# One decoder layer with 32 experts: two parked weight loads in place of one, a shorter path through routing, gates behind bank reads, the output phase on four PSUM banks

## The chip, the cores and the metric

The kernel runs on one core of a Trainium2 chip. The metric is the device time of one execution in microseconds (us). A core has TensorE for matmuls (PE; its loads of the stationary operand are shown as PEld), VectorE (DVE), ScalarE (ACT), GpSimd (POOL) and SyncE (SP). Here SP does nothing but issue the big weight transfers, in the order of its program, each when the buffer it writes is free. A label such as SPq means the sequencer of that engine. All numbers are float32, so the work is dominated by reading some 450 MB of weights.

## The reference, cut to what matters

```python
mod = silu(c) @ w_ada + b_ada                      # six (D,) vectors a sequence: sh1 sc1 g1 sh2 sc2 g2
h = rms_norm(x, norm1_g) * (1 + sc1) + sh1         # 256 prompt tokens, 8 sample tokens, D = 1024
hq, hf, hi, hg, gq, gk, gv, gg, gr = split(h @ w_in)   # HGRN2 and GLA heads
o_h = rms_norm(gated_recurrence(silu(hq), k_h, hi, log_f)) * silu(hg)
o_g = rms_norm(gated_recurrence(gq, gk, gv, log_a)) * silu(gg)
x = x + g1 * (concat(o_h, o_g) @ w_o)
h = rms_norm(x, norm2_g) * (1 + sc2) + sh2
logits = h @ router_w + router_b                   # 32 experts, top 4
gate = softmax(top 4 logits)
y = sum over the 4 experts e of gate_e * (act(h @ w_up[e] + b_up[e]) @ w_down[e] + b_down[e])
x = x + g2 * y                                     # then the final rms_norm
# w_up: 32 x 1024 x 2048, w_down: 32 x 1024 x 1024; act is a clamped SwiGLU
```

## The kernel before, in words

There are two parts. The **front** (everything up to the first expert) computes the conditioning vectors, the projections, the two recurrences, the output projection and the routing. The **experts** are then done one after the other, with all tokens of an expert gathered into one block of 64 columns: 56 prompt tokens and the 8 sample tokens.

**Buffers.** Weights go through `ring`, 128 partitions by 16 slots of 2048 numbers. The front uses them as single slots of 1 MB (`FRONT` is the order of its 42 loads, `FRONT_SLOT` their slots); the experts use them as 8 pair slots of 2 MB. An expert has 6 loads of 2 MB: four of `w_up` (256 rows each) and two of `w_down`. They are numbered in the order in which PE uses them: loads 0 to 3 are expert 0's `w_up`, and then each step n has `w_up` blocks 0 and 1 of expert n+1, both `w_down` blocks of expert n, and `w_up` blocks 2 and 3 of expert n+1. So load i of the experts can be issued when the load that held its slot has been used: `reuse(i)` on SP (line 493) waits for that. The upper 8 single slots of the ring serve the front as scratch (`scr`: attention, states, sample states), and are free only when the front's output phase has read them and the sample states are stored (load 2 waits for both).

**The parked load.** Load 8 (`ASIDE`) does not go to the ring. `load_aside` (line 510) writes it in four parts of 512 KB to free pieces of the tensor `arena`, once the output heads are normalised (`on_ready` 4). So nine loads are in place or on their way when PE starts on expert 0. Load 9 is the first that reuses a slot; it is issued in three parts as PE goes through load 0 (`load_parts`, line 519). After that, load 16 and before wait for the load nine earlier, and all later ones for the load eight earlier.

**The order of the front.** `MIDDLE` (line 84) is a list written out by hand: `proj` (a projection of 128 output rows), `ada` (a part of the conditioning product, one slot), `lev` (a level of the chunked recurrence), `vs`/`vt` (values turned), `sam`/`samt`/`kdt`/`state` (sample outputs, keys turned, states), `out`. PE, ACT and DVE each walk through it. Results of `lev`, `vs`, `vt` and so on go through three PSUM banks in turn (`aux_bank()`, `AUX_BANK`), and PE waits for DVE to have read a bank three uses earlier (`aux_used`). For the gates (projections HG and GG) ACT computes a sigmoid in a slow chain of activations (lines 754, 755, 691, 692), and DVE multiplies (line 1753, `take_gates_open`) ahead of whatever the next task asks of it. The 32 up biases are turned by 16 small transposes on PE (line 1121, task `bup`) after the first HQ projection.

**The output phase** (task `out`, lines 1208 to 1231): PE multiplies values by attention for the HGRN2 heads (two banks), then for the GLA heads (two banks); `ostat` (line 1079) sums the squares that ACT made, ACT makes the inverse root (lines 834, 836), DVE normalises (line 1873, `on_ready`), and PE goes through `w_o` (line 1293). Then DVE adds to the residual (`x1_ready`), ACT squares, PE does the router (lines 1312, 1341) and turns the tokens (line 1303).

**Routing and the first expert.** DVE takes the top four of each token (lines 1918 to 1926: maxima, their indices, four one-hot rows a token, summed to `picked` at line 1931), PE counts ranks (lines 1357 and 1360), DVE makes the pick matrix (line 1948), PE gathers the tokens (line 1379), ACT copies, PE turns (line 1388), DVE adds the shift (line 1961), and `up` (line 1408) begins. `keep_going(7)` (line 1351) are matmuls without a use while PE waits. `rows` (line 1259) turns the vector g2 in two halves around the first turn.

**An expert step** on PE: gather, `back` (line 1426), `turn`, `combine` (line 1449), `up` blocks 0 and 1, `gates`, `down` (line 1462), `up` blocks 2 and 3. The steps stand in loops of four with `PEEL` = 3 ahead, and step `MIDDLE_AT` = 15 has the down biases. State loads, sample values and state stores are issued by POOL; small vectors and `b_up` by ACT.

## Time and profile before

| | |
|---|---|
| median of 3 runs | 1181.11 us (1179.96 to 1181.35) |
| the profiled execution | 1180.3 us, its span 1178.5 us |
| PE busy | 1118.9 us (95%) |
| DVE busy | 413.6 us (35%) |
| ACT busy | 191.0 us (16%) |
| moved by DMA | 460.96 MB, 391 GB/s over the span |
| mean granted clock of PE | 0.988 |

The span runs from the first to the last instruction. All times of rows are from its start. Matmuls are pipelined and their ends are modelled, so PE "busy" in these tables doesn't say that it is at its limit. The DMA rate in 40 equal slices, the chain of waits, and the issues of the transfers say more here than the busy shares do.

### The profile page before, as it was taken

Reading aid. Unit: us, or ns where it says so; the run is one execution under the profiler, and the core shown is the slowest. Engines: PE = TensorE matmul, PEld = TensorE weight load, DVE = VectorE, ACT = ScalarE, POOL = GpSimd, SP = SyncE. Lnnn points to the kernel's source line nnn. Section 1 sums busy time; section 2 is a strip of 40 time slices with the busy share of each in tenths; the row PEclk is TensorE's granted clock in tenths of the full one; section 3 lists DMA queues with packets and bytes.
Section 4 is the critical chain, followed back from the end, with each engine's and each line's share of the span. In section 5 each row is a group of like instructions: output and inputs, shape, how many; then the busy total and the mean of one; then the engine's idle time right before and its main releaser. Section 6 shows DMA issues by size and latency. Waiting matters only on the chain.

```text
span 1178.5 us, 14278 instructions
## 1 busy us (share of the span) xinstructions
PE 1118.9 (95%) x5652; PEld 499.4 (42%) x5652; DVE 413.6 (35%) x847; ACT 191.0 (16%) x384; POOL 29.2 (2%) x59
## 2 busy tenths in 40 slices
PE   6999998999999999999999989999999999999996
PEld 4777676763333333333333333333333333333332
DVE  3135552352333333333333343333333333333324
ACT  2161222221111111111111111111111111111112
POOL 0201010000000000000000000000000000000001
PEclk8999999999999999999999999999999999999999
DMA  9998994879999999999999999999999999999995
GB/s 348 360 309 220 355 288 156 356 263 408 392 428 429 428 427 428 427 428 429 429 429 429 428 427 427 429 428 426 428 428 427 429 427 428 428 430 427 427 428 207
DMA packets 51178, 460.96 MB, mean 391 GB/s; under 512 B 7012, under 2 KB 7984, under 8 KB 24472
## 3 DMA queue, kind: packets, MB, share of 16 engines
q1 hardware_dynamic: 44864, 449.66, 92.3%
q0 software_dynamic: 2752, 9.47, 3.3%
q10 hardware_dynamic: 3512, 1.14, 0.4%
q8 instruction: 34, 0.56, 0.2%
q14 instruction: 16, 0.13, 0.0%
HBM read 455.60 MB, written 4.65 MB: 391 GB/s over the span
## 4 chain that ended last, share of the span: by engine, by line
PE 64%; DMA 26%; DVE 1%; ACT 1%; issue 0%; ACTq 0%; DVEq 0%; SPq 0%
PE bank L1408 25%; DMA ring<-in_w_up 23%; PE bank L1462 13%; PE bank L1058 5%; PE bank L1449 5%; PE bank L1379 3%; DMA ring<-in_w_down 3%; PE bank L1293 3%; PE bank L1426 2%; PE bank L1022 1%; PE bank L1388 1%; PE bank L1178 1%; PE bank L1437 1%; PE bank L1155 1%; PE bank L1259 1%
## 5 line engine op out<-in xcount | busy, mean ns | idle before, releaser
L1408 PE MATMUL bank<-ring,arena 128*64 128x512 f32 x2032 | 452.6, 595 | 26.4 <-DMA ring<-in_w_up 25.0
L1408 PEld LDWEIGHTS bank<-ring,arena 128*64 128x64 f32 x2032 | 141.4, 137 | 328.1 <-issue 276.9
L1462 PE MATMUL bank<-ring,arena 128*64 128x512 f32 x1024 | 227.2, 595 | 1.6 <-DMA ring<-in_w_down 1.6
L1462 PEld LDWEIGHTS bank<-ring,arena 128*64 128x64 f32 x1024 | 70.8, 137 | 135.7 <-issue 132.8
L1058 PE MATMUL bank<-arena,ring 128*128 128x264 f32 x448 | 109.2, 399 | 2.7 <-DMA ring<-in_w_in 1.9
L1058 PEld LDWEIGHTS bank<-arena,ring 128*128 128x128 f32 x448 | 85.2, 195 | 20.6 <-issue 3.8
L2022 DVE COPY arena<-bank 128x512 f32<-128x512 f32 x32 | 22.1, 691 | 204.2 <-PE bank L1408 204.2
L881 ACT ACTIVATE arena<-bank 128x512 f32<-128x512 f32 x32 | 19.1, 598 | 445.7 <-PE bank L1408 445.7
L2076 DVE TENSOR_TENSOR arena<-bank,arena 128x512 f32<-128x512 f32 x32 | 22.1, 691 | 189.4 <-PE bank L1462 189.4
L1449 PE MATMUL bank<-arena 64*128 64x512 f32 x256 | 80.7, 627 | 0.8 <-issue 0.8
L2071 DVE TENSOR_TENSOR arena<-arena,bank 128x512 f32<-128x512 f32 x128 | 79.1, 680 | 5.4 <-PE bank L1449 5.4
L2031 DVE TENSOR_TENSOR arena<-bank,bupT 128x512 f32<-128x512 f32 x64 | 43.9, 686 | 70.7 <-PE bank L1426 70.7
L1379 PE MATMUL bank<-arena,before 128*64 128x512 f32 x256 | 60.4, 592 | 0.0
L1954 DVE TENSOR_TENSOR arena<-before,arena 128x256 f32<-128x256 f32 x32 | 13.6, 426 | 119.4 <-PE bank L1437 119.4
L896 ACT ACTIVATE arena<-bank 128x256 f32<-128x256 f32 x32 | 12.3, 383 | 217.6 <-PE bank L1437 217.6
L1426 PEld LDWEIGHTS bank<-ident,arena 128*128 128x128 f32 x256 | 33.3, 209 | 25.8 <-issue 25.1
L1449 PEld LDWEIGHTS bank<-arena 64*128 64x128 f32 x256 | 30.5, 185 | 29.8 <-issue 17.7
L1426 PE MATMUL bank<-ident,arena 128*128 128x128 f32 x256 | 39.3, 296 | 0.5 <-ACT arena L881 0.5
L1379 PEld LDWEIGHTS bank<-arena,before 128*64 128x64 f32 x256 | 18.3, 137 | 36.0 <-issue 36.0
L1293 PE MATMUL bank<-arena,ring 128*128 128x264 f32 x128 | 30.5, 400 | 0.5 <-DVE arena L1873 0.5
L887 ACT ACTIVATE arena<-arena 128x512 f32<-128x512 f32 x32 | 20.2, 630 | 58.3 <-DVE arena L2036 58.3
L1293 PEld LDWEIGHTS bank<-arena,ring 128*128 128x128 f32 x128 | 24.9, 196 | 5.8 <-issue 1.5
(327 smaller groups left out, 679.8 us busy)
## 6 DMA issues: line engine op xcount, KB each, us to landing
ring<-in_w_up SPq DMA_DIRECT2D x126, 2048.0 KB, 31.2
ring<-in_w_down SPq DMA_DIRECT2D x63, 2048.0 KB, 29.0
ring<-in_w_ada SPq DMA_DIRECT2D x16, 1024.0 KB, 14.7
ring<-in_w_in SPq DMA_DIRECT2D x14, 1024.0 KB, 15.7
ring<-in_w_ada SPq DMA_DIRECT2D x16, 512.0 KB, 11.3
ring<-in_w_o SPq DMA_DIRECT2D x4, 1024.0 KB, 14.1
ring<-in_state_hgrn POOLq DMA_DIRECT2D x4, 512.0 KB, 14.4
arena<-sample_values POOLq DMA_DIRECT2D x4, 512.0 KB, 14.4
```

The source lines that it names most:

```text
L887: act.activation(te, tg, ACT.Exp, scale=-ALPHA).then_inc(sem("glu_step"), 1)
L1058: last = mm(bank[:, proj_bank(n), 0:T], ring[:, slot, 512 * (k % 4) + P * i:512 * (k % 4) + P * i + P], hT[:, k, :], start=(k == 0), stop= ...
L1293: last = mm(bank[:, WO_BANK[m % 3], 0:T], ring[:, FRONT_SLOT[ld], D * (k % 2) + P * m:D * (k % 2) + P * m + P], oT[:, k, :], start=(k == 0 ...
L1379: last = mm(bank[64 * half:64 * half + 64, 6, :], pick[:, i, :], h2tok[:, i, 512 * half:512 * half + 512], start=(i == 0), stop=(i == 1))
L1408: last = mm(bank[64 * half:64 * half + 64, b, :], xe[:, par, k % 4, k // 4, :], src[:, 512 * half:512 * half + 512], start=(k == 0), stop= ...
L1426: last = tr(bank[:, 2 + b, P * j:P * j + P], us[:, c0:c0 + 4 * P - 3:4], ident[:, :])
L1449: mm(bank[:, b, :], gT[64 * half:64 * half + 64, P * i:P * i + P], ysb[64 * half:64 * half + 64, :], start=True, stop=True).then_inc(sem(" ...
L1462: last = mm(bank[64 * half:64 * half + 64, b, :], acts[:, k, :], pairs[:, slot, D * kk + 512 * half:D * kk + 512 * half + 512], start=(k = ...
L2022: v.tensor_copy(us[:, 512:1024], bank[:, 1, :]).then_inc(sem("us_dve"), 1)
L2031: return TT(dst.rearrange("p (j h s) -> p j h s", j=4, h=2), bank[:, 2 + b, :].rearrange("p (j h s) -> p j h s", j=4, h=2), bias(b).to_bro ...
L2071: TT(y, y, bank[:, b, :], ALU.add).then_inc(sem("acc_used"), 1)
L2076: TT(ysb, bank[:, b, :], g2h, ALU.mult).then_inc(sem("ysb_ready"), 1)
```

## The change

Ten loads are in place or on their way ahead of expert 0 in place of nine: two parked loads (8 and 9), and two more later (18 and 19) in the same places. The second place is new: `more`, 12 KB a partition, and one piece of `arena`. Three of its four parts are issued right behind the front's loads, the fourth once `w_o` is done. The place in SBUF comes from arrays made smaller and from the descriptor space of POOL's DMAs, which goes to 4096 bytes a partition. With it: `bup` is done in the first `ada` loads, ten matmuls without a use follow there (`EARLY_FILL`); DVE takes gates after the bank reads of the recurrence's tasks; the output phase has a fourth bank; the g2 rows are turned ahead of `w_o`; top four goes by replacing the four maxima and comparing; the sample path of the residual has its own semaphore; `PEEL` is 4 and `MIDDLE_AT` 16.

```diff
-PEEL, UNROLL = 3, 4
-MIDDLE_AT = 15
+PEEL, UNROLL = 4, 4
+MIDDLE_AT = 16
...
-          + [("proj", HQ, 0), ("bup",), ("proj", HQ, 1), ...
-             ("proj", HI, 0), ("ada", 1, 0), ("proj", HI, 1), ("ada", 1, 1), ("lev", 0, 0),
-             ("proj", HI, 2), ("ada", 1, 2), ("lev", 0, 1), ...
+MIDDLE = ([("bup",)] + [("proj", HF, i) for i in range(4)] + [("proj", HQ, 0), ("proj", HQ, 1), ...
+             ("proj", HI, 0), ("ada", 1, 0), ("proj", HI, 1), ("ada", 1, 1), ("proj", HI, 2), ("lev", 0, 0),
+             ("ada", 1, 2), ("lev", 0, 1), ...
-WO_BANK = [AUX_BANK[(AUX_AT[("out",)] + 1) % 3], 1, 2]
+BUP_BANK = 5
+EARLY_FILL = 10
+OUT_BANK = [AUX_BANK[(AUX_AT[("out",)] + _n) % 3] for _n in range(3)] + [5]
+WO_BANK = [OUT_BANK[1], 1, 4]
-ASIDE = UPS + UP_FIRST + DOWNS
+ASIDE_AT = UPS + UP_FIRST + DOWNS
+FIRST_REFILL = ASIDE_AT + 2
+ASIDES = (ASIDE_AT, ASIDE_AT + 1, FIRST_REFILL + PAIRS, FIRST_REFILL + PAIRS + 1)
 def ring_place(i):
-    return i - (i > ASIDE)
+    return i - sum(i > a for a in ASIDES)
 def load_ahead(i):
     r = ring_place(i) - PAIRS
-    return r + (r >= ASIDE)
+    return next(j for j in range(r, r + len(ASIDES) + 1) if j not in ASIDES and ring_place(j) == r)
...
+        more = sb("more", [P, 3, 1024])
-        aside = [[r_gv[:, 0:1024], r_gv[:, 2112:3136]], [r_qf[:, 2048:3072], r_s[:, 512:1536]]]
+        aside = [[r_gv[:, 0:1024], r_gv[:, 2112:3136], r_qf[:, 2048:3072], r_s[:, 512:1536]],
+                 [more[:, 0, :], more[:, 1, :], more[:, 2, :], r_gv[:, 1024:2048]]]
... SP
                     if i == UPS + UP_FIRST:
-                        load_aside()
-                    if i == ASIDE:
+                        sp.wait_ge(sem("on_ready"), 4)
+                        sp.wait_ge(sem("S2_out"), 48)
+                        load_aside(ASIDES[0])
+                    if i == ASIDES[0]:
+                        sp.wait_ge(sem("logit_psum"), 1)
+                        load_aside(ASIDES[1], (3,))
+                    if i in ASIDES[:2]:
+                        continue
+                    if i in ASIDES:
+                        name, value = expert_released(ASIDES[ASIDES.index(i) - 2], 0)
+                        sp.wait_ge(sem(name), value)
+                        load_aside(i)
                         continue
                     reuse(i, q)
-                    if i == ASIDE + 1:
-                        load_parts(i, 1, k)
+                    if i == FIRST_REFILL:
+                        load_parts(i, 2, k)
+            load_aside(ASIDES[1], (0, 1, 2))
             for i in range(UPS):
... ACT
+            act.dma_start(bup, a["b_up"][0]).then_inc(sem("bup_in"), 16)      # right behind the vec loads
-                if task[0] == "proj" and task[1] in (HG, GG):
+                if task[0] == "proj" and task[1] in (HG, GG) and task != ("proj", GG, 3):
                     sigmoid(gexp[:, g % 3, :], sem("gsig_ready"))
...             # in the output phase, behind the squares of the HGRN2 heads
+                    sigmoid(gexp[:, 7 % 3, :], sem("gsig_ready"))
... PE
-            for j in range(4):
+            for j in range(3):
                 ada_half(0, j)
+            pe.wait_ge(sem("bup_in"), 16)
+            ... 16 transposes to BUP_BANK
+            ada_half(0, 3)
             ada_half(1, 0, (0,))
             half_back(0)
             ada_half(1, 0, (1,))
+            for _ in range(EARLY_FILL):
+                mm(bank[:, proj_bank(0), 0:P], ones[:, :], ident[:, :], start=True, stop=True)
...
-                    banks = [aux_bank(), aux_bank()]
+                    banks = [aux_bank(), OUT_BANK[3]]
...             # behind spread_d, ahead of wo_part(0)
+            pe.wait_ge(sem("aux_used"), AUX_AT[("out",)] + 1)
+            rows(OUT_BANK[0], 64, lambda k: modT[:, 40 + k, 0:1].to_broadcast([P, 64]))
...
             turn_rows(0)
-            turn_rows(1)
             router(4)
             pe.wait_ge(sem("sq_ready"), KT)
             row_stats(KT - 1).then_inc(sem("stat_psum"), 1)
+            turn_rows(1)
+            pe.wait_ge(sem("sq_ready"), KT + 1)
...
-            keep_going(7)
             pe.wait_ge(sem("picked_ready"), 1)
...             # the count of tokens, the sample logits and the sample tokens leave this place
             gather(0)
-            rows(7, 64, ..., range(4))
+            samples_routed()       # sample tokens, sample logits, counts
             turn(0)
-            rows(7, 64, ..., range(4, KT))
+            keep_going(4)
... DVE
+            dve.wait_ge(sem("aux_psum"), 1)
+            od.did(v.tensor_copy(bupT..., bank[:, BUP_BANK, :]), sem("aux_used"))     # ahead of modulate(0)
             for task in MIDDLE:
-                take_gates_open()
+                if kind not in ("vs", "vt", "lev", "sam", "samt", "kdt", "state", "out"):
+                    take_gates_open()
                 ... the task's own work
+                if kind in ("vs", "vt", "lev", "sam", "samt", "kdt", "state"):
+                    take_gates_open()
             def top_four(tiles):     # after v.max
-                    od.did(v.max_index(top_i[:, i, :], top_v[:, i, :], logit[:, i, :]))
+                    od.did(v.match_replace(replaced[:, i, :], top_v[:, i, :], logit[:, i, :], -ABOVE))
-                od.link(v.tensor_copy(top_f...)); a one-hot product for each tile; od.settle()
+                od.link(TT(picked[:, own, :], logit[:, own, 0:NE], replaced[:, own, 0:NE], ALU.not_equal), sem("picked_ready"))
-            od.link(v.tensor_reduce(picked..., onehot...), sem("picked_ready"))
... launch
-    nc = bacc.Bacc("TRN2", target_bir_lowering=False, num_devices=1)
+    nc = bacc.Bacc("TRN2", target_bir_lowering=False, num_devices=1, dynamic_dma_scratch_size=4096)
```

`logit` has four columns more that hold 3e38: with them, the eight maxima that DVE finds are these four and the top four, so `match_replace` replaces just these in a copy.

## Rows read from the trace of the kernel before

**Rows 1.** The page: DMA rate in 40 equal slices of the span.
```profile
GB/s 348 360 309 220 355 288 156 356 263 408 392 428 429 428 427 428 427 428 429 429 429 429 428 427 427 429 428 426 428 428 427 429 427 428 428 430 427 427 428 207
```
**Rows 2.** Windows: length, busy PE, PEld, DVE, ACT, POOL, granted clock, DMA share, GB/s.
```profile
180.00:190.00 10.00, 8.54 (x62) 7.37 (x61) 4.31 (x11) 2.61 (x8) 0.00 (x0) 1.00 0.00 1
400.00:500.00 100.00, 100.00 (x468) 37.09 (x466) 35.48 (x62) 13.87 (x24) 0.00 (x0) 1.00 1.01 428
```
**Rows 3.** The chain that ended last: start, length, what it was.
```profile
531.66 30.65 DMA ring<-in_w_up
...
1121.70 35.74 DMA ring<-in_w_down
1157.58 3.65 PE bank L1462 x16
```
**Rows 4.** SP's issues of expert loads: start, length, line, what, count.
```profile
208.87 2.01 SPq L493 DMA_DIRECT2D ring<-in_w_up  x4
...
238.22 0.33 SPq L493 DMA_DIRECT2D ring<-in_w_down  x1
...
253.00 2.90 SPq L526 DMA_DIRECT2D ring<-in_w_up  x3
...
357.97 0.33 SPq L493 DMA_DIRECT2D ring<-in_w_down  x1
```
**Rows 5.** Issue to landing of single loads: issued at 303.6 (first), at 357.97 (second).
```profile
ring<-in_w_down SPq DMA_DIRECT2D x1, 2048.0 KB, 7.7
...
ring<-in_w_down SPq DMA_DIRECT2D x1, 2048.0 KB, 13.3
```
**Rows 6.** PE in order of time, early; in brackets idle before, and releaser.
```profile
24.59 3.89 PE L1058 MATMUL bank<-arena,ring 128*128 128x264 f32 x8 [1.87 <-DMA ring<-in_w_in]
...
30.06 2.05 PE L1058 MATMUL bank<-arena,ring 128*128 128x264 f32 x8
...
49.96 2.10 PE L1121 MATMUL bank<-ident,ring 32*128 32x32 f32 x16
...
73.42 2.02 PE L1164 MATMUL bank<-arena 128*128 128x128 f32 x16 [1.17 <-ACT arena L778]
```
**Rows 7.** PE and DVE, the recurrence with its gates.
```profile
147.68 1.11 PE L1155 MATMUL bank<-arena 64*128 64x64 f32 x16 [1.25 <-DVE ring L1799]
148.71 5.51 PE L1058 MATMUL bank<-arena,ring 128*128 128x264 f32 x16
...
161.91 2.19 DVE L1813 SCALAR_TENSOR_TENSOR ring<-arena,ring 128x128 f32<-128x128 f32 x8 [3.88 <-DMA arena<-sample_values]
...
181.94 0.66 PE L1187 MATMUL bank<-ident,arena 128*128 128x128 f32 x4 [1.46 <-DVE arena L1791]
```
**Rows 8.** ACT and PE in the output phase.
```profile
194.76 0.39 ACT L754 ACTIVATE ring<-bank 128x264 f32<-128x264 f32 x1 [6.75 <-issue]
...
198.03 0.91 PE L1229 MATMUL bank<-ring 128*128 128x128 f32 x6 [2.40 <-DVE arena L1864]
...
200.11 3.47 PE L1079 MATMUL bank<-arena,ones 128*128 128x512 f32 x4
...
206.81 3.40 PE L1293 MATMUL bank<-arena,ring 128*128 128x264 f32 x8 [0.54 <-DVE arena L1873]
```
**Rows 9.** DVE and PE in routing and ahead of expert 0.
```profile
244.92 0.60 DVE L1931 TENSOR_REDUCE picked<-arena 128x64 f32<-128x256 f32 x1
...
246.26 0.61 PE L1360 MATMUL bank<-picked,ones 128*128 128x32 f32 x4
...
251.02 1.09 PE L1259 MATMUL bank<-ident,modT 128*64 128x128 f32 x8
```
**Rows 10.** Transfers of ACT and POOL (KB, us to landing); ACT scales sample states.
```profile
ring<-in_b_up ACTq DMA_DIRECT2D x1, 256.0 KB, 5.9
...
ring<-in_state_hgrn POOLq DMA_DIRECT2D x4, 512.0 KB, 14.4
...
79.55 2.45 ACT L797 ACTIVATE ring<-ring,arena 128x128 f32<-128x128 f32 x8
```

More of the change, by code:

```diff
@@ L83 @@
 HF, HQ, HI, HG, GQK, GV, GG = 1, 0, 2, 3, 4, 5, 6
-MIDDLE = ([("proj", HF, i) for i in range(4)]
-          + [("proj", HQ, 0), ("bup",), ("proj", HQ, 1), ("proj", HQ, 2), ("proj", HQ, 3),
-             ("proj", HI, 0), ("ada", 1, 0), ("proj", HI, 1), ("ada", 1, 1), ("lev", 0, 0),
-             ("proj", HI, 2), ("ada", 1, 2), ("lev", 0, 1), ("proj", HI, 3), ("ada", 1, 3), ("lev", 0, 2), ("low",), ("vs", 0),
+MIDDLE = ([("bup",)] + [("proj", HF, i) for i in range(4)]
+          + [("proj", HQ, 0), ("proj", HQ, 1), ("proj", HQ, 2), ("proj", HQ, 3),
+             ("proj", HI, 0), ("ada", 1, 0), ("proj", HI, 1), ("ada", 1, 1), ("proj", HI, 2), ("lev", 0, 0),
+             ("ada", 1, 2), ("lev", 0, 1), ("proj", HI, 3), ("ada", 1, 3), ("lev", 0, 2), ("low",), ("vs", 0),
              ("proj", GQK, 0), ("vt", 0), ("ada", 1, 4), ("lev", 0, 3), ("proj", GQK, 1), ("ada", 1, 5), ("y", 0), ("y", 1), ("lev", 0, 4),
@@ L837, in _ @@
             od.settle()
+            act.wait_ge(sem("rows_psum"), 1)
+            od.did(A(g2h, bank[:, OUT_BANK[0], :], ACT.Copy), sem("rows_sb"))
             act.wait_ge(sem("on_ready"), 4)
@@ L1034, in _, with aux_bank @@
             pe.wait_ge(sem("head_sb"), 2)
-            for j in range(4):
-                ada_half(0, j)
+            aux = [0]
+            def aux_bank():
+                b = AUX_BANK[aux[0] % 3]
+                if aux[0] >= 3:
+                    pe.wait_ge(sem("aux_used"), aux[0] - 2)
+                aux[0] += 1
+                return b
+            for j in range(3):
+                ada_half(0, j)
+            pe.wait_ge(sem("bup_in"), 16)
+            for k in range(16):
+                c0 = 512 * (k // 4) + k % 4
+                last = tr(bank[:, BUP_BANK, 32 * k:32 * k + 32], bup[:, c0:c0 + 4 * P - 3:4], ident[0:NE, 0:NE])
+            last.then_inc(sem("aux_psum"), 1)
+            aux[0] += 1
+            ada_half(0, 3)
             ada_half(1, 0, (0,))
@@ L1115, in _ @@
                     ada_back(task[1])
-                elif kind == "bup":
-                    pe.wait_ge(sem("bup_in"), 16)
-                    b = aux_bank()
-                    for k in range(16):
-                        c0 = 512 * (k // 4) + k % 4
-                        last = tr(bank[:, b, 32 * k:32 * k + 32], bup[:, c0:c0 + 4 * P - 3:4], ident[0:NE, 0:NE])
-                    last.then_inc(sem("aux_psum"), 1)
                 elif kind in ("vs", "vt"):
@@ L1389, in turn, with up @@
                 last.then_inc(sem("turned"), 1)
-            def up(par, k0, k1, loads, rounds, first=False, parts=False):
+            def up(par, k0, k1, loads, rounds, first=False, parts=None):
                 for s in range(k0, k1):
                     slot = loads(s)
-                    if slot is None:
-                        pe.wait_ge(sem("aside_in"), 64)
+                    if slot < 0:
+                        pe.wait_ge(sem("aside_in"), rounds(s))
                     else:
                         pe.wait_ge(sem(f"pair{slot}"), rounds(s))
-                    if parts and s == UPS - 1:
+                    if s == parts:
                         pe.wait_ge(sem("parts_in"), 32)
@@ L1579, in _ @@
             total = LOADS * NE
-            full = [16 * sum(expert_slot(m) == expert_slot(OVER_FIRST + i) for m in range(total) if m != ASIDE) for i in range(LOADS)]
+            full = [16 * sum(expert_slot(m) == expert_slot(OVER_FIRST + i) for m in range(total) if m not in ASIDES) for i in range(LOADS)]
             pe.wait_ge(sem("table_ready"), 1)
```

177 lines of the change are left out of this document (80 added, 97 removed).

## The prediction

> **What bounds the kernel now.** I read the DMA rate over the span first [rows 1]. From the tenth of its 40 slices on (each 29.5 us) it stays at 427 to 430 GB/s but for the last; the full rate is 428 [rows 2], so a 2 MB load takes 2.097 MB / 428 = 4.90 us. Ahead of that stand slices of 156, 220, 263 and 288. Second, the chain of waits: from 252 us to 531 it is all PE, then pieces of 30 to 35 us of "DMA ring" come in, and the end is a DMA: the last `w_down` releases PE at 1157.6 and 20.9 us follow [rows 3]. So PE is the quicker of the two over the experts, catches up with the transfers at about 531, and from there the time is that of the transfers. The last moment at which DMA had nothing to do sets the end: remaining bytes / 428, plus the 20.9 us. Nothing that PE does between 310 and 1120 us counts, only what lets SP issue loads sooner ahead of that.
>
> Third, SP's issues [rows 4]. Loads 2 to 5 go at 208.9 (they wait for the output phase), 6 and 7 at 238.2 and about 240 (for `w_o`), 9 at 253.0 (for expert 0's first matmuls). DMA idles in between: 10 us of 180 to 190 have 1 GB/s [rows 2]. The last idle is at 302 to 306: load 18 is issued at 303.6 and lands 7.7 us later, which is what a load takes when next to nothing is queued ahead of it. Load 30, at 357.97, takes 13.3 us [rows 5]: a queue stands, and doesn't go again.
>
> **Part 1, two parked loads and two more later.** With ten loads ahead in place of nine, load 10 takes the place in time that load 9 had, and so on: each lands one load's time (4.90 us) sooner against the same PE. The gap at 303.6 goes too, since load 18 now waits for load 8, used one `up` block earlier. All this lasts only up to load 27; from load 28 on, eight places are left and load 30 again waits for load 22, which PE has used at 357.97. Without queue its landing is at the earliest 7.7 us after its issue, in place of 13.3. So the gain is capped there: 13.3 − 7.7 = 5.6 us [rows 5]. Capacity without the cap would give 4.90 plus some 2 for the gap, 6.9; so the cap decides, and DMA idles once more near 358 for about a microsecond. The parts are of 4 KB a partition row in place of longer ones and come as four issues; I take off 0.4. Gain 5.2, between 3.5 and 6.9.
>
> Is there time to place ten? Three parts (1.5 MB, 3.7 us) go into the hole at 180 to 190, where nothing ran. Load 8, and the fourth part behind a wait for the router's matmuls, stand in SP's queue ahead of load 10. If all is 12 to 13 us earlier (below), loads 6 and 7 are issued at 226 and need 7.7 + 4.9, the part 1.2: about 240, and load 10 can be issued at 253.0 − 12.7 = 240.3. It just fits.
>
> **Part 2, the front moved forward.** Each microsecond by which PE reaches expert 0, and with it loads 0 to 22, sooner moves load 30 and the end by the same, as the cap is PE's own time. By stages:
>
> Early. The 16 transposes leave a stretch where PE never waits: 2.10 us [rows 6]. They go where PE waits for `ada` loads anyway. Their price is there: 256 KB more ahead of the front's loads, 0.6 us; and a wait for `bup_in`, hidden as that transfer took 5.9 us when it was issued among others [rows 10] and PE comes to it some 12 us after issue; without that cover each microsecond late counts. DVE's copy stands ahead of `modulate(0)` while it waits for PE. Eight projection matmuls take 3.89 us at half clock, just behind a 1.87 us wait, and 2.05 later [rows 6]: if `EARLY_FILL` closes that idle, 1.8 come back, but the loads of that stretch land only slightly ahead of their use, so I take 1.7 − 0.6 = 1.1, between −0.6 and 2.4. Then `lev 0 0` behind projection HI 2: the 1.17 us wait for ACT [rows 6] goes, though DVE now has one `ada` in place of a projection to do its part; 1.0, between 0 and 1.2. Sum 4.2.
>
> On that fill a rule speaks against the change in part. TensorE is at 1.2 GHz in that stretch (granted clock half) behind idle. The Trainium skill, "TensorE: Matmul & The Clock Gate", Part 4: PE-mode transpose, says a transpose doesn't count as busy for the clock the way a matmul does. By that the moved transposes would guard nothing, and the ten matmuls alone would have to; were they too few, the early sum would be 2.4 in place of 4.2. No run here shows which.
>
> Gates behind banks. At 146.4 PE waits 1.25 us for bank copies that stand on DVE behind a gate, and the 16 matmuls behind it take 5.51 us where two times 2.05 is normal, so the low clock costs 1.4 more [rows 6, 7]. 2.65 could go. But at 158 to 161.9 DVE itself waits 3.88 us for sample values that POOL fetches over memory [rows 7]; that chain of transfers doesn't get shorter, and `lev 1 6` comes behind it. I take 1.7, between 0.5 and 2.65. At `samt` a wait of 1.46 goes by the same order [rows 7]; DVE's later copies keep their place behind the gate, but PE has a projection in between. 1.5. The late gate could hold ACT, whose three `gexp` places must come free: it is two projections behind, so nothing.
>
> Output phase. PE waits 2.40 us for a bank that DVE frees behind a gate [rows 8]; the fourth bank takes this away, and ACT's sigmoid of the last gate no longer stands ahead of the squares. ACT reads the last projection only at 194.76 since its DMA issues wait for DVE's state sums [rows 8], and those come sooner by the gate order, so ACT doesn't take the wait's place. The two stretches behind idle run at half clock: `ostat` 3.47 us and the first eight of `w_o` 3.40 [rows 8]. The latter is 2.05 at full clock, 1.35 less; for the former between 0 and a half, I take 1.3. Added: the g2 rows, 1 us, in a stretch where PE waited 0.54 [rows 8] for ACT and DVE: 0.5 too many. Sum 2.4 + 1.3 + 1.35 − 0.5 = 4.6, between 2 and 6.
>
> Routing. From the chain go the one-hot products and their sum (0.60 for the sum [rows 9], as much for cast and products), for one comparison; the counts' matmuls, 0.61 modelled; and half of the g2 rows that ended the wait ahead of `up`, 1.09 [rows 9], of which some 0.4 were beyond what DVE needed. Added between gather and turn: sample logits and spread, 0.5 beyond ACT's copy. About 1.4 net. Without `keep_going(7)` PE idles twice for under 1 us, and half clock over the next 3 us would cost 1.7: at four in ten, 0.7. I take 0.7, between −0.5 and 1.8.
>
> **Sum.** 4.2 + 1.7 + 1.5 + 4.6 + 0.7 = 12.7 us forward, 5.2 from capacity, 17.9. `MIDDLE_AT` 16 moves some 12 us of PE work by one step, inside the stretch that the transfers set, and costs nothing; the end's 20.9 us are as before. The profiled execution: 1180.3 − 17.9 = 1162.4; the median is 0.8 above it, so 1163.
>
> **Rivals.**
> A. The clock stays low: the idle pieces only change place (`keep_going(7)` is gone, PE waits for DVE's short steps), so 1.7, 0.9 (what is counted of the 1.4), 1.3 and 1.35 are not won, 5.2 in all: 1168. For it: each low stretch in these rows stands behind an idle of 0.5 to 2.4 us [rows 6 to 8]. Against: a 1.17 and a 1.46 us idle had none.
> B. The front's forward move is lost on its transfers: slices 2 to 6 have DMA busy throughout though at a low rate; if PE then waits for slots, capacity alone stays: 1180.3 − 5.2 + 0.8 = 1176. Against: behind 25 us PE waits for no load in the front.
> C. The change doesn't do what it says: the tenth load lands in time that was busy, and PE's part is eaten by waits of DVE: no difference, 1181. The hole at 180 to 190 speaks against it.
> D. Slower. POOL's descriptor space is cut to 4096 bytes a partition. If POOL can then have only one or so of its state loads under way, the four of 512 KB [rows 10] land one behind the other, 14.4 us each from 40.3: the fourth at 98, where ACT scales it some 4 us behind the third's 79.55 [rows 10]; the four of 256 KB follow until about 155 where ACT is at about 110. PE stalls behind ACT for some 45 us: 1181 − 18 + 45 = 1208. It decides once the delay at ACT is over 17.9 us. The Trainium skill, "SBUF — State Buffer", SBUF size: 192, 224, or 256?, calls this space a 16 KiB ring of descriptors for the software-made DMAs; by that a quarter of the ring is left. No run here shows its depth. Against: in the present trace these loads queue behind the front's anyway, and there are 20 us between landing and use.
>
> **How the numbers follow.** Forecast 1163 at 0.60, with its own range 1158 to 1169; A 0.18; B 0.10; C 0.04; D 0.05; and 0.03 for more than I count (the waits' upper bounds: 1155). Range 1157 to 1174: it leaves out C, D, half of B and most of the last. Faster by over 0.2% (2.4 us, about what a measurement tells from none): 0.91; within: 0.04; slower: 0.05.
>
> **What would show it.** First `up` matmul at about 239.5 in place of 252.1; no half clock at 23 to 30, 149 to 153 and 200 to 211; no L1155 or L1187 wait for DVE; DMA moving data right behind the front's loads; no gap at 290 to 295 and a small one near 345; PE joins the transfers two to three experts later than 531; the last load's release about 18 us sooner with 20.9 behind it. Wrong if the front is forward and the end isn't, if a DMA gap opens later than 350, or if ACT waits for states.

## The result, and the profile after

The changed kernel takes 1164.59 us (median of 4 runs, 1163.76 to 1166.47) against 1180.53 (4 runs, 1178.98 to 1181.35) of the kernel before beside it: 0.9875 of it, 95% interval 0.9855 to 0.9895. The profiled execution is 1164.73 us with a span of 1163.0, that is 15.5 less than before. The forecast was a median of 1163 and a profiled execution 17.9 us shorter.

The rate in slices, and single windows (length, busy PE, PEld, DVE, ACT, POOL, granted clock, DMA share, GB/s), answer to [rows 1, 2]:

```profile
GB/s 335 377 297 227 322 349 229 371 359 392 419 419 422 427 425 429 427 429 428 429 428 428 429 427 429 427 429 426 428 428 427 429 429 429 427 429 427 428 427 212
```
```profile
8.00:10.00 2.00, 2.00 (x8) 1.21 (x7) 0.00 (x0) 1.84 (x6) 0.00 (x0) 1.00 1.07 316
10.00:12.00 2.00, 1.67 (x6) 0.90 (x5) 1.55 (x5) 1.52 (x6) 0.00 (x0) 1.00 1.02 264
170.00:180.00 10.00, 10.00 (x150) 8.94 (x147) 3.87 (x12) 2.95 (x8) 0.00 (x0) 1.00 0.80 321
180.00:190.00 10.00, 10.00 (x72) 8.89 (x71) 4.61 (x8) 2.10 (x7) 0.00 (x0) 1.00 0.23 61
...
345.00:350.00 5.00, 5.00 (x26) 1.70 (x24) 2.43 (x5) 0.00 (x0) 0.00 (x0) 1.00 0.91 334
...
400.00:500.00 100.00, 100.00 (x466) 36.14 (x464) 31.43 (x55) 10.79 (x19) 0.00 (x0) 1.00 1.01 428
```

The hole of 10 us at 180 is not closed but moved: the three parked parts run ahead of it, at 170 to 180. The idle of the transfers at 302 to 306 is gone, and a small one is at 345 to 350: 5 × (1 − 334/428) = 1.1 us. The full rate of 428 is as before.

SP's issues of the experts' loads and the chain of waits answer to [rows 3, 4]:

```profile
162.08 4.02 SPq L524 DMA_DIRECT2D more<-in_w_up  x3
...
188.75 14.41 SPq L496 DMA_DIRECT2D ring<-in_w_up  x6
...
228.99 2.10 SPq L496 DMA_DIRECT2D ring<-in_w_down  x2
233.38 0.33 SPq L524 DMA_DIRECT2D arena<-in_w_up  x1
242.63 2.90 SPq L533 DMA_DIRECT2D ring<-in_w_up  x3
...
347.46 3.77 SPq L496 DMA_DIRECT2D ring<-in_w_down  x2
```
```profile
602.58 33.71 DMA ring<-in_w_up
...
1106.46 35.42 DMA ring<-in_w_down
1141.89 0.14 issue
1142.02 3.65 PE bank L1488 x16
```

PE joins the transfers at 602.6 in place of 531.7, and the last load lets it go at 1142.0 in place of 1157.6, with 21.0 us behind it in both. Load 30, issued at 347.46, lands after 9.8 us (13.3 before, rows 5). `b_up`, now issued within the first 5 us, lands after 8.4 (5.9 before, rows 10):

```profile
ring<-in_w_down SPq DMA_DIRECT2D x1, 2048.0 KB, 9.8
...
ring<-in_b_up ACTq DMA_DIRECT2D x1, 256.0 KB, 8.4
```

PE in order of time (start, length, line, operation; in brackets the idle before and its releaser), to be laid beside [rows 6 to 9]:

```profile
23.99 1.08 PE L1021 MATMUL bank<-ring 128*32 128x256 f32 x8 [2.25 <-DMA ring<-in_w_ada]
...
26.64 4.33 PE L1076 MATMUL bank<-ident,ones 128*128 128x128 f32 x20
30.80 1.95 PE L1095 MATMUL bank<-arena,ring 128*128 128x264 f32 x8
...
146.97 1.11 PE L1176 MATMUL bank<-arena 64*128 64x64 f32 x16
...
193.40 1.99 PE L1117 MATMUL bank<-arena,ones 128*128 128x512 f32 x4
...
199.22 2.05 PE L1316 MATMUL bank<-arena,ring 128*128 128x264 f32 x8
...
235.12 0.41 PE L1380 MATMUL bank<-picked,before 128*128 128x32 f32 x2 [0.43 <-DVE picked L1955]
...
236.88 1.94 PE L1404 MATMUL bank<-arena,before 128*64 128x512 f32 x8 [0.90 <-ACT arena L881]
...
241.51 1.07 PE L1433 MATMUL bank<-ring,arena 128*64 128x512 f32 x3
```

From 142 us to the first `up` PE has no idle of 0.4 us or more left but the two of the routing. `ostat` takes 1.99 us in place of 3.47, and the first eight matmuls of `w_o` 2.05 in place of 3.40. In the first 31 us the picture is the other way round: PE waits 2.25 us for an `ada` slot, the fill (ten matmuls in 20 records, L1076) runs at half clock for 4.33 us, and the first projection starts at 30.80, where it was 24.59.

The next table cuts each profile at the first matmul of a stage, in us. "Restart" is PE's first matmul behind the second modulate (39.11 before). "Stream" goes from the first `up` to the moment when 1920 of the semaphore updates that landing transfers make were left, and "rest" from there to the last update. A load of 2 MB makes 16 of them. Some 111 weight loads are left at that moment (233 MB are still to be moved); the other updates are those of the last norm vector and of the outputs, so "rest" has the 21 us behind the last weight load in it.

| profile | restart | to `sam` | to `w_o` | to first `up` | first `up` | stream | rest |
|---|---|---|---|---|---|---|---|
| before | 39.11 | 133.70 | 34.00 | 45.04 | 251.86 | 367.16 | 559.11 |
| changed | 42.72 | 127.69 | 28.81 | 42.29 | 241.51 | 362.42 | 558.65 |
| e1 | 40.27 | 128.08 | 28.81 | 43.99 | 241.15 | 362.59 | 559.15 |
| e2 | 36.77 | 129.93 | 28.81 | 42.29 | 237.80 | 362.74 | 558.15 |
| e3 | 36.95 | 129.92 | 28.81 | 43.90 | 239.58 | 362.46 | 559.09 |
| e4 | 39.45 | 127.69 | 28.81 | 43.97 | 239.92 | 361.32 | 560.69 |
| e5 | 40.81 | 127.95 | 28.81 | 43.99 | 241.56 | 367.05 | 559.41 |
| e6 | 41.93 | 128.92 | 30.48 | 42.30 | 243.63 | 362.67 | 560.86 |
| e7 | 41.90 | 127.70 | 29.18 | 44.00 | 242.78 | 362.32 | 560.50 |
| e8 | 38.87 | 127.69 | 28.81 | 44.97 | 240.34 | 362.53 | 558.92 |
| e9 | 41.32 | 127.69 | 28.81 | 43.98 | 241.81 | 362.61 | 559.19 |
| e10 | 37.90 | 133.70 | 33.39 | 45.04 | 250.03 | 366.91 | 559.50 |
| e11 | 38.63 | 127.70 | 28.81 | 42.29 | 237.42 | 362.62 | 559.32 |
| e12 | 37.70 | 129.93 | 28.81 | 42.31 | 238.74 | 362.30 | 560.47 |

Three things can be read off. First, the 15.5 us are 10.35 of front, 4.7 of stream and 0.5 of rest. Second, the stages in the middle repeat well for one front: to 0.4 us from the restart to `sam`, to 0.01 from there to `w_o` in the changed one (0.6 in that of before), and to 0.02 from `w_o` to the first `up` but for a stretch of low clock of 1.7 us, treated below. So single profiles tell edits there apart. The restart (37.9 to 39.1 for the front of before, 38.6 to 42.7 for that of the change) doesn't repeat.

Third, the rest takes anything from 558.2 to 560.9. That is no slower rate. Counted in the bytes of the traces' DMA packets, the way from 230 MB left to 20 MB left takes 490.7 to 490.8 us in all fourteen profiles. The difference comes behind it: from 20 MB left to the landing of the last whole 2 MB load it is 39.6 us in e2 and 41.4 in e7, and at that landing 3.05 MB and 2.31 MB are still to come. So in e7 more of what is queued behind the load has been moved by the time its last piece lands. What holds that piece back wasn't tried. In e6 another 1.7 us come behind that landing (22.8 us to the end in place of 21.1), where the granted clock is low. By all this a difference of under 2 us between the ends of two profiles says nothing about an edit, and medians too move by about that: the changed kernel has 0.9875 of the kernel before here, and 0.9894 in e11.

### The profile page after: what moved, and what is told of

It reads as the page before. It is cut to its first block, busy times and chain, and to the rows that moved or that the text cites. A ratio compares the mean times of both kernels' runs of the same rounds, so it can differ in the third digit from the quotient of the medians.

```text
span 1163.0 us, 14304 instructions
## 1 busy us (share of the span) xinstructions
PE 1115.0 (96%) x5666; PEld 498.6 (43%) x5666; DVE 411.7 (35%) x841; ACT 191.1 (16%) x385; POOL 28.7 (2%) x57
## 4 chain that ended last, share of the span: by engine, by line
PE 75%; DMA 22%; SPq 1%; DVE 1%; ACT 1%; issue 0%; DVEq 0%; ACTq 0%
PE bank L1433 28%; DMA ring<-in_w_up 18%; PE bank L1488 15%; PE bank L1095 9%; PE bank L1474 5%; PE bank L1404 4%; DMA ring<-in_w_down 3%; PE bank L1316 2%; PE bank L1451 2%; PE bank L1040 1%; DMA ring<-in_w_ada 1%; PE bank L1413 1%; PE bank L1199 1%; PE bank L1462 1%; SPq L473 1%; PE bank L1176 1%
## 5 line engine op out<-in xcount | busy, mean ns | idle before, releaser
L1433 PE MATMUL bank<-ring,arena 128*64 128x512 f32 x2016 | 448.2, 595 | 21.5 <-DMA ring<-in_w_up 20.2
L1433 PEld LDWEIGHTS bank<-ring,arena 128*64 128x64 f32 x2016 | 139.8, 137 | 320.1 <-issue 277.7
L1488 PE MATMUL bank<-ring,arena 128*64 128x512 f32 x992 | 220.1, 595 | 1.3 <-DMA ring<-in_w_down 1.3
L1488 PEld LDWEIGHTS bank<-ring,arena 128*64 128x64 f32 x992 | 68.6, 137 | 131.3 <-issue 129.1
L1095 PE MATMUL bank<-arena,ring 128*128 128x264 f32 x448 | 105.4, 390 | 0.8 <-DVE arena L1695 0.8
L1095 PEld LDWEIGHTS bank<-arena,ring 128*128 128x128 f32 x448 | 83.1, 190 | 17.9 <-issue 4.5
L1474 PE MATMUL bank<-arena,gpickT 64*128 64x512 f32 x248 | 78.7, 628 | 0.0
L916 ACT ACTIVATE gpickT<-bank 128x256 f32<-128x256 f32 x31 | 11.9, 384 | 217.6 <-PE bank L1462 217.6
L1474 PEld LDWEIGHTS bank<-arena,gpickT 64*128 64x128 f32 x248 | 29.8, 185 | 27.7 <-issue 15.6
L1316 PE MATMUL bank<-arena,ring 128*128 128x264 f32 x128 | 29.2, 388 | 0.0
L1316 PEld LDWEIGHTS bank<-arena,ring 128*128 128x128 f32 x128 | 24.1, 190 | 5.0 <-issue 1.1
```

What stands on the lines that cost most here:

```text
L1095: last = mm(bank[:, proj_bank(n), 0:T], ring[:, slot, 512 * (k % 4) + P * i:512 * (k % 4) + P * i + P], hT[:, k, :], start=(k == 0), stop= ...
L1316: last = mm(bank[:, WO_BANK[m % 3], 0:T], ring[:, FRONT_SLOT[ld], D * (k % 2) + P * m:D * (k % 2) + P * m + P], oT[:, k, :], start=(k == 0 ...
L1433: last = mm(bank[64 * half:64 * half + 64, b, :], xe[:, par, k % 4, k // 4, :], src[:, 512 * half:512 * half + 512], start=(k == 0), stop= ...
L1474: mm(bank[:, b, :], gT[64 * half:64 * half + 64, P * i:P * i + P], ysb[64 * half:64 * half + 64, :], start=True, stop=True).then_inc(sem(" ...
L1488: last = mm(bank[64 * half:64 * half + 64, b, :], acts[:, k, :], src[:, 512 * half:512 * half + 512], start=(k == 0), stop=(k == KT - 1))
```

## The experiments

Each experiment was run beside the kernel before, in three groups: e1 to e4 (before 1180.41, 1174.69 to 1182.53), e5 to e8 (before 1175.99, 1172.17 to 1185.68), e9 to e12 (before 1177.08, 1173.04 to 1179.48). Ratios are to the kernel before of the same group, with a 95% interval. All but e10 are edits of the changed kernel.

### The early step: fill and b_up

**e1**: no fill (`EARLY_FILL = 0`). **e2**: `b_up`'s transfer and transposes where they were. **e3**: both.

```diff
 e1, e3
-EARLY_FILL = 10
+EARLY_FILL = 0
 e2, e3
-MIDDLE = ([("bup",)] + [("proj", HF, i) for i in range(4)]
-          + [("proj", HQ, 0), ("proj", HQ, 1), ...
+MIDDLE = ([("proj", HF, i) for i in range(4)]
+          + [("proj", HQ, 0), ("bup",), ("proj", HQ, 1), ...
...
```
In e2 and e3 the issue on ACT, the 16 transposes on PE and DVE's copy move back with the task.

> The changed kernel without the ten matmuls of EARLY_FILL. Theory: they lie in the half-clock stretch at 23.7 to 30.5 us, take 4.33 us and end 3 us after the data they wait beside; without them the first projection starts at about 27.3 in place of 30.8 (itself still at half clock), the second `modulate` and all behind it come about 1.6 us sooner, and so does the end: span 1161.4 in place of 1163.0. Rival: without them the half clock lasts one more stretch of 6.8 us, the projections from 30 to 37 double, and the kernel gets 1 to 3 us slower (1164 to 1166).

> The changed kernel with the up biases as before: transfer issued at about 36 us, 16 transposes behind projection HQ 0; the ten matmuls stay. Theory: the early transfer of 256 KB is what brings the second halves of the `ada` loads 2 to 3 us late; undone, the first projection starts at about 27 (behind the fill) in place of 30.8, and the 2.1 us of transposes come back at 50: first `up` 1.7 us sooner, span about 1161.3. Rival: the lateness is not from that transfer (it costs its 0.6 us only): then the span gets about 1.5 us longer, 1164.5.

> Both undone: up biases as before and no EARLY_FILL. Theory: the front up to 39 us is that of the kernel before (second hT ready for PE at 39.1 in place of 42.7), less the 2.1 us of transposes: 1.5 us sooner than the changed kernel, span 1161.5. If the fill holds the clock once it is in time (rival), the kernel of e2 is quicker than this one by up to 1.8 us; if it only takes time, it is slower by up to 1.

Measured: e1 1162.7 (ratio 0.9852, 0.9816 to 0.9887), e2 1161.68 (0.985, 0.9813 to 0.9887), e3 1163.45 (0.986, 0.9825 to 0.9896). The medians don't part them; the stages do. PE's first pieces in e2, with fill and late `b_up`:

```profile
20.70 0.64 PE L1021 MATMUL bank<-ring 128*32 128x256 f32 x8 [1.27 <-DMA ring<-in_w_ada]
...
22.20 2.50 PE L1070 MATMUL bank<-ident,ones 128*128 128x128 f32 x20
24.54 1.95 PE L1089 MATMUL bank<-arena,ring 128*128 128x264 f32 x8
...
36.77 5.58 PE L1089 MATMUL bank<-arena,ring 128*128 128x264 f32 x24 [0.82 <-DVE arena L1695]
```

The same 20 records take 2.50 us at full clock and 4.33 at half. Late `b_up` puts the restart at 36.77, 36.95 and (e12) 37.70, without half clock in all three; early `b_up` at 39.45, 38.87 and 38.63 (e4, e8, e11) where there was none either. So the early transfer and transposes cost 38.98 − 37.14 = 1.8 us on the mean of three, and the transposes give back 129.93 − 127.69 = 2.2 later: early `b_up` gains 0.4 net. The landings show where the 1.8 go: the second halves of the first five `ada` slots land at 9.8, 12.5, 15.2, 18.0 and 20.7 us in e2, and at 12.2, 14.9, 17.6, 20.3 and 24.0 in the changed kernel. The fifth lands at 20.7 to 21.5 us in all five profiles with late `b_up` (e10 and the kernel before among them) and at 22.8 to 24.4 in all nine with the early one. Behind full clock the fill gives nothing: e2 and e3 are 0.2 apart. Where the clock has fallen it costs: e1, without it, has its restart at 40.27, about as much sooner as was expected (1.6) than the mean of the others with half clock (41.7).

Half clock at 21 to 30 us came in the changed kernel, e1, e5, e6, e7 and e9, and not in e4, e8 and e11. The front up to there is the same in all nine, but for e1's fill; e11 is the changed kernel itself. With half clock and the fill the restart is 40.8 to 42.7, mean 41.7, so the two cost 41.7 − 39.0 = 2.8 on the mean. It isn't the length of the idle ahead alone: behind 1.27 us it came in e5 and not in e11, and e3 had two idles of 1.64 and 1.69 without it.

### Capacity

**e4**: a third pair of parked loads (`PEEL = 8`, six entries in `ASIDES`). **e5**: nine loads ahead in place of ten, the rest as changed.

```diff
 e4
...
+          FIRST_REFILL + 2 * PAIRS + 2, FIRST_REFILL + 2 * PAIRS + 3)
 e5
-FIRST_REFILL = ASIDE_AT + 2
+FIRST_REFILL = ASIDE_AT + 1
-ASIDES = (ASIDE_AT, ASIDE_AT + 1, FIRST_REFILL + PAIRS, FIRST_REFILL + PAIRS + 1)
+ASIDES = (ASIDE_AT,)
...
```

> The changed kernel with two more parked loads, 28 and 29, in the same places (PEEL 8). Theory: the gain of the ring is capped where load 30 has to wait for load 22 (issued 347.46, landed 9.8 us later, 352 GB/s at 346 to 348 and 262 at 348 to 350); with the third pair the small hole at 346 to 350 goes, and the span is about 1 us shorter, 0.5 to 1.5: 1162.0. Rival: the hole is no idle time of the transfers but how a load starts, or another hole opens behind 38: no change, 1163.0.

> The changed kernel with one parked load (8) as before: load 9 refills the first slot in parts, nothing goes to `more`. The front is untouched. Theory: from the first `up` matmul to the end the changed kernel takes 921.5 us and the kernel before 926.7; with nine loads it is 926.7 again, so with the first `up` at 239.9 to 241.5 the span is 1166.6 to 1168.2. Rival: the forward front already filled the hole that the tenth load would use, or the holes behind 290 are of another cause: the span from the first `up` stays under 923.

e4: 1164.82 (0.9874, 0.9835 to 0.9913). e5: 1169.46 (0.9932, 0.9907 to 0.9957). Windows of e4, then of e5:

```profile
345.00:350.00 5.00, 5.00 (x26) 1.64 (x24) 1.27 (x4) 0.39 (x1) 0.00 (x0) 1.00 1.06 442
```
```profile
290.00:300.00 10.00, 10.00 (x48) 3.27 (x46) 4.05 (x8) 0.39 (x1) 0.00 (x0) 1.00 0.87 336
```

With nine loads the idle of before is back ahead of 300, and the stream with it: 367.05, as before's 367.16. Ten loads give 362.42 in the changed kernel and up to 362.74 elsewhere, so capacity is worth 4.3 to 4.7 us, apart from everything else in the change. Counted in bytes, from the first `up` to 230 MB left, it is 374.5 to 374.6 us with nine and 369.8 to 370.0 with ten: 4.6. e4 closes the hole at 345. Its stream is 1.1 us shorter, but counted in bytes it is 0.8 to 1.0 us ahead of the others just behind the hole (340 MB left) and only 0.4 to 0.5 at 230 MB left. Its rest happened to be 560.69, so that neither the end nor the median shows a gain.

### Gates and the output phase

**e6**: DVE takes gates ahead of the bank reads, as before. **e7**: three banks in the output phase.

```diff
 e6
-                if kind not in ("vs", "vt", "lev", "sam", "samt", "kdt", "state", "out"):
+                if kind != "out":
 e7
-                    banks = [aux_bank(), OUT_BANK[3]]
+                    banks = [aux_bank(), aux_bank()]
...
```

> The changed kernel with DVE taking the gates ahead of each task of the recurrence, as before (the output phase stays new). Theory: the waits of 1.25 us (L1155, at the first gate) and 1.46 us (at `samt`) come back, the fixed chain of the sample values hides part of the first, and ACT's read of the last projection moves back: from the restart of the projections at about 40 us to the first `w_o` matmul it takes 159.6 us in place of 156.5, 3 us more, and the end is 3 us later. With the low clock behind the first wait it could be 4.7. Rival: the order does nothing and the output phase's new bank took the gain: 0.

> The changed kernel with three PSUM banks for the output phase: the fourth product goes to the first bank again, once DVE has read it; the g2 rows go to bank 5. Theory: PE idles between the HGRN2 and the GLA products, about 1.5 us (2.4 before, less what ACT's later sigmoid and the gate order gave), and at times the clock falls behind it (3 us more). From `sam` to the first `w_o` matmul 28.8 us become 30.3, or 33 with the low clock. Rival: ACT has squared and DVE has read the bank by then, and nothing changes: 28.8.

e6: 1167.02 (0.991, 0.9881 to 0.9939); e7: 1166.21 (2 runs; 0.9898, 0.9826 to 0.997). e6 brings back both waits of [rows 7]:

```profile
147.40 1.11 PE L1176 MATMUL bank<-arena 64*128 64x64 f32 x16 [1.15 <-DVE ring L1826]
...
179.98 0.66 PE L1208 MATMUL bank<-ident,arena 128*128 128x128 f32 x4 [1.45 <-DVE arena L1818]
```

They cost 128.92 − 127.69 = 1.2 and 30.48 − 28.81 = 1.7 us, this time without the low clock that followed the first of them before. e10 below has the front of before, and shows the same: behind the same wait as in [rows 7] its 16 matmuls take 3.83 us at full clock, where the kernel before took 5.51, so that stretch of low clock cost 1.7 us, and it came by chance:

```profile
148.15 1.11 PE L1155 MATMUL bank<-arena 64*128 64x64 f32 x16 [1.25 <-DVE ring L1799]
149.18 3.83 PE L1058 MATMUL bank<-arena,ring 128*128 128x264 f32 x16
```

With the rest of the change in place, the fourth bank is worth only 29.18 − 28.81 = 0.4. So nearly all of the wait of 2.40 us [rows 8] is gone with three banks too, and what else changed there is DVE's order and the sigmoid that no longer stands ahead of the squares. These two were not parted, and no run has the fourth bank without them.

### Does the end follow the first up, and only that

**e8**: 16 useless matmuls in place of 4 just ahead of the first `up`. **e9**: 16 useless matmuls in each of the steps 7, 11 and 15.

```diff
 e8
-            keep_going(4)
+            keep_going(16)
 e9
+                if n0 == 7:
+                    keep_going(16)
                 up(par, 0, UP_FIRST, lo, ro, parts=0 if n0 == 1 else None)
```

> The changed kernel with 16 in place of 4 matmuls without a use right ahead of the first `up`: PE's 250 ns each, 12 more, 3.0 us. Theory: the end is tied to PE's release of load 22, so the whole span grows by these 3.0 us, and the 921.5 us from the first `up` to the end stay. Rival: the end is set by transfers alone whose order is fixed by then, and ten loads in place give cover: the span grows by under 1 us and the 921.5 shrink.

> The changed kernel with 16 useless matmuls in each of the steps 7, 11 and 15 of the experts (3 x 16, about 3.5 to 4 us for each group at full clock, 11 us in all), whose results nothing uses. Theory (the experts' stage waits for the weights' transfers, and TensorE has time to spare up to the point where it joins them for good, 602.6 us in the changed kernel): the time from the first up matmul to the end stays at 921.5 us, within 1 us, and the span at 1163. Rival (these steps are already TensorE's own time, so each useless matmul is paid): the same stretch takes 932, the span 1174. Between the two: steps 7 and 11 free and step 15 paid, 925.

e8: 1167.42 (0.9914, 0.9886 to 0.9942). e9: 1165.58 (2 runs; 0.9906, 0.9877 to 0.9935). PE's rows of e8, then one of the three groups of e9:

```profile
236.68 3.74 PE L1375 MATMUL bank<-ident,ones 128*128 128x128 f32 x32
240.34 1.94 PE L1433 MATMUL bank<-ring,arena 128*64 128x512 f32 x8
```
```profile
452.50 3.84 PE L1375 MATMUL bank<-ident,ones 128*128 128x128 f32 x32
```

In e8 the matmuls make the way to the first `up` 44.97 − 42.29 = 2.7 longer, and the stream behind it is the same (362.53): the end follows one to one. (Its profiled execution is no longer than the changed kernel's, since its restart was 3.85 us sooner; its median, 0.9914 of the kernel before, shows the delay.) In e9 11.5 us of work between 452 and 681 leave the stream at 362.61 and the rest at 559.19: it costs nothing, although PE has no idle of 0.4 us or more from 263 to 717 there. This is the plainest proof that PE's 96% busy isn't the bound.

### The descriptor space

**e10**: the kernel before with `dynamic_dma_scratch_size=4096` and nothing else.

> The kernel before with the descriptor space of 4096 bytes and nothing else of the change. Rival D of the prediction (the smaller space makes GpSimd's or VectorE's DMAs wait for room): later landings of the state loads and a span above 1190. Theory (none of this kernel's DMAs comes near that space): 1178.5 span, median 1180 with the kernel before, the state loads landing as before, within 0.3 us each.

1179.05 (8 runs) against 1177.08 (15 runs): 1.0017, 0.9999 to 1.0035. The rows of POOL's issues in e10:

```profile
39.03 2.86 POOL L629 DMA_DIRECT2D ring<-in_state_hgrn  x3 [35.10 <-DVE arena L1668]
48.13 0.90 POOL L629 DMA_DIRECT2D ring<-in_state_hgrn  x1 [6.23 <-issue]
49.01 0.70 POOL L629 DMA_DIRECT2D ring<-in_state_gla  x1
50.78 1.37 POOL L629 DMA_DIRECT2D ring<-in_state_gla  x2 [1.07 <-issue]
54.41 0.68 POOL L629 DMA_DIRECT2D ring<-in_state_gla  x1 [2.26 <-issue]
```

Before, the eight went out in one go from 40.2 to 46 us. Now the fourth waits 6.2 us for nothing that the profile shows, and so do later ones (in the changed kernel it is 7.2, 2.8 and 3.2). So the smaller space does hold POOL back, after three loads of 512 KB, and the theory that nothing comes near it fell, as did its 0.3 us. The landings in the trace say how: the first load lands at 47.8 us and the fourth is issued at 48.1, the second at 50.5 and the sixth at 50.8; in the changed kernel the first lands at 53.6 and the fourth is issued at 53.9. But the last state load lands at 72.0 us in e10 and 74.4 before, and from the restart to `sam` both take 133.70, each with one stretch of low clock of 3.4 us in it: no cost that I can show. The interval of the ratio has 1 in it.

In e10 that stretch is at 51.5 us, and it is the only one in the front of any profile with no wait in the 10 us ahead of it. PE has no idle of 0.35 us or more from 37.9 us on; the 16 transposes of `b_up` end just ahead of the fall, and the projections behind them are slow:

```profile
48.74 2.10 PE L1121 MATMUL bank<-ident,ring 32*128 32x32 f32 x16
50.78 11.52 PE L1058 MATMUL bank<-arena,ring 128*128 128x264 f32 x43
```

### The changed kernel again, and a version pointed to

**e11** is the changed kernel once more. **e12** has late `b_up` as e2, and fills the two waits of the routing:

```diff
 e12
+            keep_going(3)
             pe.wait_ge(sem("picked_ready"), 1)
...
+            keep_going(4)
             gather(0)
```

> The changed kernel once more, beside the next one on the same chip: 1163 to 1165 us, 0.987 to 0.99 of the kernel before. Its first low-clock stretch (23.7 us, 3.3 us long in its price) comes in some executions and not in others, so that its profile may show the first matmul behind the modulate at 39.5 or at 42.7 us.

> The changed kernel with b_up's transfer and transposes at their old places and with 3 and 4 filling matmuls put back ahead of the two waits that follow the routing, where the prediction's kernel has none and a low-clock stretch of 3.4 us came at about 234 us in five of the nine profiles. Theory: restart behind the second modulate at 36.9 us (42.7 in the changed kernel), from there to the first sampling matmul 129.9 (127.7), from the first w_o matmul to the first up 42.3 with no low clock at 234, the first up matmul at 238 to 239 and the end at 1160, so a median of 1161, about 3 us under the changed kernel beside it. Rival (the fill costs its own length on the path and the low stretch comes anyway): from w_o to the first up 44 to 45, first up at 240.5, a median of 1163 to 1164, the same as the changed kernel.

e11 1163.47 (1161.59 to 1165.19; 0.9894, 0.9873 to 0.9915), e12 1162.6 (1161.76 to 1164.44; 0.9882, 0.9861 to 0.9903): not to be told apart. e12's first `up` is at 238.74 us, as its theory had it, and the end 1.9 us later than its 1160, as the rest took 560.47. The two waits are gone in e12, and the fill costs nothing there (42.31 against 42.29):

```profile
233.03 1.14 PE L1375 MATMUL bank<-ident,ones 128*128 128x128 f32 x8
234.10 1.94 PE L1405 MATMUL bank<-arena,before 128*64 128x512 f32 x8
```

In e1, by contrast, behind the same idle of 0.90 as in the changed kernel:

```profile
234.82 3.62 PE L1404 MATMUL bank<-arena,before 128*64 128x512 f32 x8 [0.90 <-ACT arena L881]
```

That is 1.7 us, paid in e1, e3, e4, e5, e7 and e9, not in the changed kernel's first profile, e2, e6, e8 and e11: six of eleven. One profile of e12 can't show that the fill prevents it. That its median isn't 3 us lower fits what the stages say: moving `b_up` back loses 0.4 us and doesn't win 3, and the low clock at 21 to 30 us comes only in some executions. The theory of 3 us was built on the changed kernel's one unlucky profile.

## Why the prediction was right

The time and the mechanism were right: the end is PE's arrival at expert 0 plus a stretch set by transfers (e8, e9, e5). That the number came so near is in part luck: of the 12.7 us forward the early step missed 4.8, and the other stages gave 2.5 more than forecast, in good part because the stretches of low clock that the kernel before had in its profile were dearer than forecast, and one of them comes only by chance. Term by term, in the order of the prediction:

- **Capacity, 5.2 forecast, 4.6 to 4.7 measured** (e5 against the changed kernel), and the small idle that was expected near 345 is there with 1.1 us. One detail was too kind: load 30 lands after 9.8 us and not 7.7, as load 31 goes right behind it.
- **Early, 4.2 forecast, about 0.6 lost in the first profile** (3.6 later at the restart, against 2.2 and 0.8 won behind it). This is the one step that failed. Of its parts, the transposes (2.1) gave 2.2. The wait of `lev 0 0` went, 1.17, for one of 0.38 on DVE at 80.5 us: 0.8 of the 1.0. But "256 KB more ahead of the front's loads, 0.6 us" was mis-sized: it is 1.8 on the mean and 2.4 to 3.3 in the landings of the `ada` slots, three to five times its share of bytes. In the windows of 8 to 12 us the rate is 316 and 264 GB/s, where the kernel before has 381 and 392 there, while the busy share of the DMA engines is the same (1.07 and 1.02 against 1.03 and 1.05): they work, but move less. Why a transfer of 32 rows of 8 KB slows the others so much was not tried. And the half clock, 1.7 to be won by the fill, stayed: the fill stands behind the idle that it was to guard, so where the clock has fallen, the fill itself runs at half speed and takes up to 1.9 us more.

  The Trainium skill, "TensorE: Matmul & The Clock Gate", Part 4: PE-mode transpose, would have the moved transposes guard nothing; by that the sum was to be 2.4. The traces agree in that nothing was guarded, but e2 and e3, with and without fill and with the transposes at their old place, had no half clock there at all. e10's low stretch right behind the 16 transposes, with no wait ahead, speaks for the rule; but it came in one of the five profiles that have the transposes at that place, so no run parts the rule from chance.
- **Gates, 1.7 forecast, 3.0 measured.** From restart to `sam` the change wins 6.0: 2.2 are the transposes, 0.8 `lev 0 0`, and 3.0 are left for the gates. e6 gives 1.2 for the wait alone. The low clock behind it [rows 7] was put at 1.4 and is worth 1.7 (5.51 us against e10's 3.83 behind the same wait). That part is luck: e6 and e10 have the wait without it. The cap that I set for the sample values did not bind in the changed kernel, where PE has no wait there; in e1 and e5 it cost 0.59 and 0.45 us, and their way to `sam` is longer by 0.4 and 0.3.
- **`samt` 1.5, output phase 4.6 less 1.35 of `w_o`'s clock: 4.7 forecast, 5.2 measured.** 1.7 of them came by `samt`'s order (e6), 1.7 by the clock of `ostat` (from its start to the router's matmuls 5.5 us before and 3.8 now; 1.3 forecast), and the g2 rows took 0.8 back (0.5 forecast). The 2.40 us of the bank wait went as forecast, but most of it doesn't need the fourth bank: with three, 0.4 comes back (e7).
- **`w_o` to first `up`: 1.35 for the clock and 0.7 for the routing forecast, 2.75 measured.** From the start of `w_o` to its ninth matmul it takes 5.48 us before and 3.83 now, so the clock gave 1.65, as the low stretch went on behind the first eight; 1.1 are left for the routing, where 1.4 were counted without a low clock. The 1.7 us at four in ten was a fair price: six of eleven profiles paid it, the changed kernel's did not.
- **`MIDDLE_AT` and PE's work inside the stream, nothing forecast, nothing measured** (e9).

So 12.7 forward became 10.35; had the profile been e11, it would have been 251.86 − 237.42 = 14.4, more than forecast. Of rival A (clock stays low) one place of four came true, and the routing's new waits brought another low stretch in some executions. Rival B had the right mechanism for the early step, PE waiting for slots, but it took about 2 us, not 12.7. C is excluded by the result, and its tenth load in busy time by e5. D was a real mechanism with no price: the issues stop after three loads, not after one or so, and nothing that the stages show waits for them.

## What to carry to other kernels

In a kernel whose end is set by transfers, find the last moment at which they are idle. What moved PE ahead of it here moved the end one to one, and what was added behind it was free as long as PE had time to spare, however busy it looked. Put a fill for the clock ahead of or inside the wait; behind it, it ran at half clock itself and only cost time. A small transfer put ahead of a stream that PE is already waiting for can cost several times its bytes; read it from the landings of what stands behind it. And cut one execution into stages before you compare: most stages in the middle repeat to a few hundredths of a microsecond, where medians of the same kernel differ by 2.

## What the runs showed of the hardware

- The granted clock fell to half at 20.7 to 23.7 us in six of nine executions of nearly the same program, and at 233.8 to 236.5 us in six of eleven, behind the same idles of 0.43 and 0.90 us in all eleven. A stretch of 3.4 us at half clock cost 1.7.
- Once, in e10, it fell with no wait ahead, right behind 16 transposes of 32 × 32 (at 51.5 us); the other four profiles with the same transposes at that place show no fall.
- The bulk of the weight loads, from 230 MB to 20 MB left, took 490.7 to 490.8 us in all fourteen executions. The last 20 MB up to the landing of the last whole load took 39.6 to 41.4 us, and this is where the ends part.
- With 4096 bytes of descriptor space GpSimd issues three loads of 512 KB and holds the fourth for 6.2 us (e10) and 7.2 (the changed kernel), until 0.3 us behind the landing of the first; with the space of before it issued all eight loads without a break.
- A transfer of 256 KB that took 8.4 us beside a stream of 512 KB loads put the landings of that stream back by 2.4 to 3.3 us.
